# Two-block transformer on one core: the adaptive shift leaves the first three projections and comes back as a bias

## The reference, cut to what matters

```python
mod = (silu(c) @ w_ada + b_ada)            # 6 x 1024 values from one vector c
shift1, scale1, gate1, shift2, scale2, gate2 = split(mod, 6)
h = rms_norm(x, norm1_w) * (1.0 + scale1) + shift1
proj = h @ w_in                            # 11 column blocks of 256, and 16 gate columns
gq, gk, gv, gz, ga, gb, sq, sk, sv = split(proj, ...)
qkv = silu(causal_depthwise_conv(concat([gq, gk, gv]), conv_w))   # four taps
# gated delta rule on q, k, v; sliding window attention on sq, sk, sv; w_out; residual
```

## Time and profile before

| | |
|---|---|
| median of 3 runs | 989.45 us (989.44 to 989.48) |
| profiled execution, its own time | 991.1 us |
| its span | 989.3 us |
| PE busy | 977.1 us |
| DVE busy | 607.5 us |
| ACT busy | 476.9 us |
| DMA, mean over the span | 188 GB/s |

### The profile page before, as it was taken

The page is one execution under the profiler, slowest core; times in us unless marked ns, Lnnn a source line. Parts: engine busy times, 40 slices in busy tenths (PEclk is TensorE's granted clock), DMA queues, the critical chain, the costliest instruction groups (busy, mean ns, idle before and its releaser), DMA issues.

```text
span 989.3 us, 15628 instructions
## 1 busy us (share of the span) xinstructions
PE 977.1 (99%) x6703; PEld 845.5 (85%) x6703; DVE 607.5 (61%) x750; ACT 476.9 (48%) x640; POOL 36.8 (4%) x37
## 2 busy tenths in 40 slices
PE   8999999999999999999999999999999999999998
PEld 6799989978888888999888888889999888888886
DVE  2688987775665454787754545365876663545444
ACT  3485377454343435533364344446655563435343
POOL 0000560010000000000000000000000000000000
PEclk9999999999999999999999999999999999999999
DMA  9857224775767354446544645454643435554621
GB/s 345 310 183 266 97 87 149 272 241 217 276 217 289 129 209 173 169 173 213 213 144 155 213 171 207 176 194 147 231 153 129 140 145 184 182 202 166 217 85 43
DMA packets 31588, 185.70 MB, mean 188 GB/s; under 512 B 3040, under 2 KB 5536, under 8 KB 10784
## 3 DMA queue, kind: packets, MB, share of 16 engines
q1 hardware_dynamic: 29984, 180.37, 50.9%
q0 software_dynamic: 832, 3.17, 1.0%
q10 hardware_dynamic: 704, 1.17, 0.3%
HBM read 183.62 MB, written 1.07 MB: 187 GB/s over the span
## 4 chain that ended last, share of the span: by engine, by line
PE 96%; DVE 2%; DMA 1%; ACT 0%; issue 0%; SPq 0%; DVEq 0%
PE bank L1708 50%; PE acc L1708 42%; PE bank L2313 1%; DMA X_inv<-stream 1%; PE bank L2091 1%; PE bank L1804 0%; PE acc L1804 0%; PE acc L2091 0%; PE bank L2171 0%; SPq L566 0%; DVE norm_tmp L1125 0%; PE bank L1984 0%; DVE inv_b L1393 0%; DVE norm_tmp L1513 0%; DVE silu_and_hid L1512 0%
## 5 line engine op out<-in xcount | busy, mean ns | idle before, releaser
L1076 DVE TENSOR_TENSOR w_lo<-raw,w_hi 128x2048 fp32r<-128x2048 f32 x144 | 326.9, 2288 | 146.7 <-ACT w_hi L676 146.6
L1708 PE MATMUL bank<-w_hi,h_parts 128*128 128x512 f32 x1056 | 333.5, 391 | 1.3 <-DVE h_parts L1154 1.3
L676 ACT ACTIVATE w_hi<-raw 128x2048 fp32r<-128x2048 f32 x144 | 271.4, 1909 | 101.8 <-PE acc L1708 70.9
L1708 PEld LDWEIGHTS bank<-w_hi,h_parts 128*128 128x128 f32 x1056 | 198.2, 188 | 44.6 <-issue 1.9
L1708 PE MATMUL bank<-w_lo,h_parts 128*128 128x512 f32 x528 | 205.5, 389 | 0.0
L1708 PE MATMUL acc<-h_parts,w_hi 128*128 128x256 f32 x928 | 169.6, 285 | 1.8 <-DVE h_parts L1129 0.9
L1708 PEld LDWEIGHTS acc<-h_parts,w_hi 128*128 128x128 f32 x928 | 142.1, 188 | 6.7 <-issue 3.3
L1708 PE MATMUL acc<-h_parts,w_lo 128*128 128x256 f32 x464 | 130.5, 281 | 0.0
L1708 PE MATMUL acc<-w_hi,o_hi 128*128 128x512 f32 x296 | 119.1, 402 | 0.0
L1708 PEld LDWEIGHTS bank<-w_lo,h_parts 128*128 128x128 f32 x528 | 99.2, 188 | 19.8
L1708 PE MATMUL acc<-w_hi,o_lo 128*128 128x512 f32 x296 | 115.6, 391 | 0.0
(11 more groups left out here) (370 smaller groups left out, 992.4 us busy)
## 6 DMA issues: line engine op xcount, KB each, us to landing
raw<-stream SPq DMA_DIRECT2D x162, 1024.0 KB, 5.1
AT<-stream SPq DMA_DIRECT2D x2, 1024.0 KB, 12.2
qkT<-stream SPq DMA_DIRECT2D x2, 1024.0 KB, 13.4
X_inv<-stream SPq DMA_DIRECT2D x2, 1024.0 KB, 14.3
keys_queries<-stream SPq DMA_DIRECT2D x4, 512.0 KB, 12.7
t_tables<-t_scratch POOLq DMA_DIRECT2D x1, 2048.0 KB, 10.6
x_res<-x_in SPq DMA_DIRECT2D x2, 512.0 KB, 5.1
t_tables<-t_scratch POOLq DMA_DIRECT2D x1, 1024.0 KB, 12.9
```

The source lines that it names most:

```text
L676: act.activation(high_of(w), raw_of(r), ACT.Copy).then_inc(s.hi_ready, 1)
L1076: dve.tensor_tensor(low_of(w), raw_of(weight_load(w)), high_of(w), ALU.subtract).then_inc(s.lo_ready, 1)
L1708: return pe.matmul(o, l, r, start=start, stop=stop, skip_group_check=True)
```

## The change

Since h = x * a1 + shift, h @ w = (x * a1) @ w + shift @ w, and the second term is one number per output column. Projections 0 to 2 (`BIASED`) are now made from the scaled rows without the shift, and shift @ w is added when the product is copied into the convolution's pads.

- Loads: the four pieces of scale come first, w0 and w1 between them, then w2, then the four pieces of shift. w3 and w4 (`ASIDE`) land in two of the `ada_raw` buffers. w5, w6 and w7 go into the three raw slots, each after its slot's bias product.
- `scaled_high` and `scaled_low` make the parts of x * a1; `scale_rows` keeps x * a1 itself. When the shift is there `h_high` and `first_low` overwrite the parts with those of h, for projection 3 onwards and for the gate columns.
- The first half of the shift is summed by `ada`; the second on VectorE (`accumulate_shift`, eight instructions on 128 x 512).
- `bias_part` multiplies the shift by the raw weights of w0 to w2 (six calls of four matmuls), two copies on ScalarE, `bias_sums`, and a copy into `bias`. `last_columns` is gone, `warm` falls from 46 matmuls to 31.
- w2 and w3 are split by quarters too. There are two pads and two convolution sums. The gate columns' product moves ahead of projection 3.
- Later: `project(8)` moves ahead of the rows `kb01`, `kb23`, `q01`; `kq_sums` 0 and 1 move into projection 7. On VectorE `accumulate` of m8, m9, m10 and m11 and `lo(10)` move as shown.

```diff
-FIRST_WEIGHTS = 2
+FIRST_WEIGHTS = 4
+BIASED = 3
+ASIDE = 2
...
+            load_ada(0)
+            load_ada(1)
             load(0)
             load(1)
-            for i in range(4):
-                load_ada(1, i)
-            sp.wait_ge(ada_landed[2], 32)
-            for i in range(2, len(LOADS)):
+            load_ada(2)
+            load_ada(3)
+            load(2)
+            for i in range(4, 8):
+                load_ada(i)
+            for i in range(3, len(LOADS)):
                 load(i)
...
+            def accumulate_shift(i):
+                dve.wait_ge(ada_landed[2 + i], 32)
+                for k in range(4):
+                    piece, c = ada_raw[2 + i][:, 512 * k:512 * k + 512], c_act[:, 4 * i + k:4 * i + k + 1]
...
+                    ins = dve.scalar_tensor_tensor(out=shift_acc, in0=piece, scalar=c, in1=shift_acc, op0=ALU.mult, op1=ALU.add)
...
+            accumulate_shift(0)
+            first_shifts(0)
+            for k in range(4):
+                first_low(k)
+            accumulate_shift(1)
             first_shifts(1)
...
+            def bias_part(w, half):
+
+                for k in range(4):
+                    ins = mm(bias_bank(w)[32 * k:32 * k + 32, :], shift_columns[:, 4 * half + k, :], raw_of(w)[:, 4 * half + k, :],
+                             half == 0 and w != 1, half == 1)
+                return ins
...
+            column_part(0, range(0, 4))
+            column_part(1, range(0, 2))
+            ada(2)
+            column_part(1, range(2, 4))
+            ada(3)
+            warm(2)
+            pe.wait_ge(s.rows_copied, 2)
+            row_sums(1, mod_rows[1])
+            column_part(2, range(0, 4))
+            ada(4)
+            column_part(0, range(4, 6))
+            ada(5)
+            column_part(0, range(6, KD)).then_inc(s.block_used, 1)
+            column_part(1, range(4, KD)).then_inc(s.block_used, 1)
+            pe.wait_ge(s.rows_copied, 3)
+            row_sums(2, mod_rows[2])
+            column_part(2, range(4, 6))
+            pe.wait_ge(s.shift_dve, 1)
+            for w in range(BIASED):
+                bias_part(w, 0)
+            pe.wait_ge(s.shift_dve, 2)
+            row_sums(3, shift_acc)
+            column_part(2, range(6, KD)).then_inc(s.block_used, 1)
+            pe.wait_ge(s.gab_lo, 1)
+            gab_part(range(0, 4))
+            pe.wait_ge(s.shift_dve, 3)
+            for w in range(BIASED):
+                bias_part(w, 1).then_inc(s.bias_product, 1)
+            gab_part(range(4, KD)).then_inc(s.gab_product, 1)
+            bias_sums()
+            column_part(3, range(0, 4))
...
-            lo(8)
             at = MOD_START[1]
-            accumulate(at)
-            at += 1
             dve.wait_ge(s.head_sums, 1)
             link(dve.tensor_scalar(hs[:, 0, :], STAT[:, 64:96], EPS, None, ALU.add))
             dve.reciprocal(hs[:, 1, :], hs[:, 0, :]).then_inc(s.head_inv, 1)
-
+            lo(9)
             hsv = hs[:, 2, :].rearrange("p (t c) -> p t c", t=TT)
             dve.wait_ge(s.head_rms, 1)
...
-            lo(9)
+            accumulate(at)
+            at += 1
...
             row_scale("q01", qT[:, 0:2, :], qT[:, 0:2, :])
-
-            accumulate(at)
-            at += 1
-            lo(10)
-            accumulate(at)
-            at += 1
             row_scale("q23", qT[:, 2:4, :], qT[:, 2:4, :])
...
             for gi in range(3):
                 decay(gi)
-
+            accumulate(at)
+            at += 1
             decay(3)
+            lo(10)
             accumulate(at)
             at += 1
...
             for gi in range(4):
                 wait_big(f"qk{gi}")
                 big_read(f"qk{gi}", dve.tensor_tensor(qkT[:, gi, :], big(f"qk{gi}")[:, :], DT[:, gi, :], ALU.mult))
+            accumulate(at)
+            at += 1
...
-            project(6, first_sums)
+            project(6)
+            project(7, first_sums)
             kq_sums(2)
             kq_sums(3).then_inc(s.head_sums, 1)
-            project(7)
+            project(8)
...
             rows("q01", at(coefq), (0, 1))
-            project(8)
             rows("q23", at(coefq), (2, 3))
```

More of the change, by code:

```diff
@@ L549, in load @@
             def load(i):
[L550 to L570, removed]
@@ L749, in feature, with pad_rows @@
                     act.activation(head_sq[w].rearrange("p (a b) -> p a b", a=2), dest[w], ACT.Square).then_inc(s.head_squared, 1)
[L751 to L754, removed]
+            def pad_rows(w):
                 act.wait_ge(s.block_used, w + 1)
[L756 to L772, removed]
@@ new lines, in pad_rows @@
+                if w >= 2:
+                    act.wait_ge(s.conv_done, w - 1)
+                if w >= BIASED:
+                    act.activation(pads[w % 2][:, :, 3:259], A[w % 4].rearrange("p (a b) -> p a b", a=2), ACT.Copy).then_inc(s.pad_ready, 1)
+                    return
+                for mt in range(2):
+                    act.activation(pads[w % 2][:, mt, 3:259], A[w][:, 256 * mt:256 * mt + 256], ACT.Identity,
+                                   bias=bias[:, 2 * w + mt:2 * w + mt + 1]).then_inc(s.pad_ready, 1)
@@ new lines, in _ @@
+            for k in range(4, KD):
+                scaled_low(k)
+            first_lows(2, (2, 3))
+            accumulate_shift(0)
[3 more added lines that the diff above has]
+            accumulate_shift(1)
+            first_shifts(1)
+            first_low(4)
+            first_low(5)
+            first_lows(3, (0, 1))
+            first_low(6)
+            first_low(7)
+            first_lows(3, (2, 3))
+            dve.wait_ge(s.rows_summed, 5)
@@ new lines, in conv @@
+                        dve.wait_ge(s.dve_step, steps[0] - 1)
+                        ins = dve.scalar_tensor_tensor(out=o, in0=pad[:, mt, tap:tap + 256], scalar=vec[:, cw:cw + 1],
+                                                       in1=o, op0=ALU.mult, op1=ALU.add)
+                        if tap == 3 and mt == 1:
+                            dve.wait_ge(s.dve_step, steps[0])
+                            ins.then_inc(s.conv_done, 1)
+                        else:
+                            ins.then_inc(s.dve_step, 1)
+                            steps[0] += 1
@@ new lines, in row_sums, with bias_sums @@
+                    ins = by_halves(STAT[:, at:at + WIDE], rows[:, P * j:P * j + P], ones.broadcast_to([P, WIDE]), True, True)
+                ins.then_inc(s.rows_summed, 1)
+            def bias_sums():
+                pe.wait_ge(s.rows_copied, 5)
+                pe.wait_ge(s.mod_ready, 4)
+                for j in range(2 * BIASED):
+                    at = WIDE * j
+                    ins = by_halves(STAT[:, at:at + WIDE], bias_rows[:, P * j:P * j + P], ones.broadcast_to([P, WIDE]), True, True)
```

433 lines of the change are left out of this document (244 added, 189 removed).

## The result

| | before | changed |
|---|---|---|
| median | 989.45 us (989.38 to 989.48, 5 runs) | 1000.16 us (999.96 to 1000.41, 5 runs) |
| span of the profiled execution | 989.3 us | 998.6 us |

The ratio is 1.0102, 95% interval [1.0091, 1.0113]: 10.7 us slower. The direction was forecast, with about half of the size (+5.4), and the time lies above the range (990.5 to 998.5).

The account below looks back on a forecast made before the run. TensorE, busy 977 of 989 us, was taken to bound the kernel; 0.7 gained at the start and delays in VectorE's list summed to +5.4, span 994.7, time 994.8. Own range 993.3 to 996.3, full range 990.5 to 998.5.

Parts of the forecast that it names:

- first product: TensorE's first product at the start, claimed at 18.0 us, six us earlier than before.
- `bias_part` at 0.45: Bias products at the start, 0.45 us each; first three covered by the shift wait, last three on the path at 1.35.
- the shift wait in place of the old one: Before the shift's row sums, TensorE waits 2.8 us for VectorE's sum of the second half, known at 46.0.
- the late w10: w10's load, issued at 90.4 instead of 83.0 once m8 frees its slot, lands 5.8 us later at 96.2.
- the wait for `eg`: ScalarE, behind `hi(10)`, reads `eg` at 99.5 instead of 98.2; VectorE's `kbgT` queues behind it, +1.2 us.
- `qk` waiting for the `kk` read: VectorE's first `kk` read at 114.8 instead of 110.65; `qk` on TensorE waits for its banks, TensorE +4.1 us.
- an unbroken tail: From the first inversion update to the end nothing is made up; the same distance as before.
- So I add nothing: Slow TensorE clock after the new waits at 43 and `qk`: priced at nothing and made a rival.
- I take the difference as the same for both.: Profiled execution 991.1, span 989.3, median 989.45: difference taken as equal for both kernels, giving span 994.7, time 994.8.
- The start: TensorE up to projection 4: shift known at 46.0, row sums 46.6, projection 4 at 60.3 against 61.0, gain 0.7.
- Then one accumulation 2.3 … one accumulation 2.3: VectorE between G2's mask (106.7) and the first `kk` read (114.8): two accumulations, each priced at 2.3 us.
- Rival 3: Slow clock after the new waits, at two or three places 0.8 to 1.7 us: 996.5 to 998.5; chance 0.2.

Follow-up runs that it names:

- run 2: Changed kernel with the shift summed in one piece, VectorE doing all eight accumulate_shift instructions before first_shifts(0) and the low parts: 997.41 us, ratio 1.0075.
- run 3: Changed kernel with VectorE's late work reordered (m8 before the head sums, m9 behind the coefficients, lo(10) behind q23, m10 before the last decay): 995.17 us, 1.0047.
- run 9: Both repairs and the first two waits filled, with one accumulation fewer before the softmax (done later), against the changed kernel: 995.91 us, 1.0060.
- run 5: Changed kernel with zero matmuls in all of TensorE's waits (6, 4, 9, 3 and 14), run twice: 997.56 and 997.43 us, the second 1.0072.
- run 6: Changed kernel with both repairs, the shift summed in one piece and VectorE's late work reordered: 990.84 us, ratio 1.0010.
- run 8: Kernel before the change without 22 zero matmuls of its start: 993.02 us, ratio 1.0041.
- run 1: Changed kernel with ten zero matmuls in the shift wait alone: 1001.75 us, ratio 1.0115.
- run 4: Changed kernel with GpSimd scaling only 4 of 512 columns of each decay block, the others left unscaled: 996.93 us, ratio 1.0070.
- 7: Changed kernel with both repairs (shift in one piece, VectorE's late work reordered) and zero matmuls in the first two waits: 990.96 us, ratio 1.0012.
- 11: Run 9 with four more zero matmuls, ahead of the square sums of w_out's last block: 992.73 us, ratio 1.0032.

## Why the forecast was half of the loss

Right, with its size: first product, `bias_part` at 0.45, the shift wait in place of the old one (2.58 for 2.8; without it, in run 2, projection 4 starts 2.4 earlier), the late w10, the wait for `eg`, `qk` waiting for the `kk` read, VectorE as the new bound (run 3: 4.1 back at the first update from the order alone; run 9), an unbroken tail. So the path was right, and what failed are terms of the sum: the clock put at nothing, twice, the start, and the price of an accumulation. Forecast and measured differ by 5.3 us, and it adds up so:

- **"So I add nothing"**, the clock after the shift wait. The spell came and cost 1.1: projection 4 at 63.0, at 61.88 with the waits filled. That after `qk` VectorE covers it was right (run 5).
- **"I take the difference as the same for both."** This is the step I had not doubted. The kernel before took 991.1 in its profiled execution and 989.45 in the median, and that 1.65 was the spell of the earlier trace rows: most later executions of it have spans of 987.6 to 988.5 at a mean clock of 0.999 to 1.000, the others 989.2 to 990.1 at 0.997 to 0.998. The changed kernel has the spell, at 156, in its trace, and its other four executions, with the same mean clock (0.994) and spans within 0.4 us, look the same. So the spans to be compared are some 987.8 and 998.3, and 1.5 was missing from the sum. What such a spell costs is seen behind the first update, too: to the end it is 859.1 to 859.4 us in the traces that have one there (before, changed, 5, 6, 8), and 857.4 to 858.0 in those that have none (1 to 4, 7).
- **The start, 1.6 too late apart from the clock**: the shift's row sums come at 47.07 in run 5 (46.0 forecast), and half a microsecond of that is there by w2's first product (29.60 for 29.1 in the changed kernel); from the row sums to projection 4 it is 14.8, not 14.3.
- **"Then one accumulation 2.3 … one accumulation 2.3"**: mis-sized. Three of them run beside GpSimd at 3.12, 3.13 and 3.30, 2.5 more; the first two, 1.6, stand ahead of the `kk` read. The four subtractions behind them, which GpSimd used to slow, take 2.48 in place of 4.20, which takes back the third and more, and w10 landed 4.9 after its slot was free, not 5.8. From projection 4 to the first update this leaves 76.1 us against 75.2 forecast.
- From the first update to the end 0.2.

Together 1.1 + 1.5 + 1.6 + 0.9 + 0.2 = 5.3. The parts are differences between single traces and spans, good to a few tenths. Rival 3 had the clock as the cause but priced the wrong places: one of its spells was hidden, and the one that counted was in my base.

On the mis-sized accumulations the Trainium skill has a rule that the forecast should have weighed: "SBUF — State Buffer", section "Who interferes with whom", says that VectorE and GpSimd share a port pair as an exclusive lock, that a VectorE instruction with two SBUF inputs contends with a GpSimd instruction that reads SBUF, and that the order of issue decides which of the two is blocked. The traces agree: a norm on GpSimd takes 1.04 where it starts first, as in run 1, where the mask of VectorE that starts 0.17 later takes 1.42 instead of 0.69,

```profile
108.43 1.04 POOL L643 TENSOR_TENSOR X_inv<-X_inv,head_stat 128x512 f32<-128x512 f32 x1 [43.58 <-ACT X_inv L880]
```

and 2.36 where it starts behind `lo(10)`. The accumulation behind `lo(10)` then starts while that norm runs and takes 3.13. In run 4 the accumulations go back to 2.35, and the one at 108.02 in the kernel before, which started first, took 2.34.

What is not settled: which wait is followed by a spell. The same wait of 1.2 us before w2 had one behind it in runs 1 and 2, none in the changed kernel and none in run 6. The shift wait of 2.6 had one behind it in the changed kernel and in run 3, none in run 4, which had one at 19 instead. That zero matmuls matter is shown (runs 5 and 8); that a given number of them at a given place is enough is not (runs 1 and 11). Why the steps of the start took longer than forecast was not tried.

## What to carry to other kernels

Before a sum is made on a profiled execution, subtract what makes it differ from the median: here a slow spell of 1.7 us stood in it, and the changed kernel kept it for good. An earlier start is worth only what the engine that binds later can take over: 1.8 us gained at projection 4 were gone 70 us later, because VectorE's convolutions had to wait for the bias and its list was pushed out of TensorE's shadow. When work is moved on VectorE, look at what GpSimd does at the new place and which of the two starts first, and when waits are removed or added, leave the zero matmuls or expect to pay for the clock.

## What was not expected of the hardware

- 22 zero matmuls left out cost 3.3 us (run 8), and one wait of 0.87 us stood ahead of 13 us at half clock (run 9). Most other spells seen here lasted some 3.4 us, that at `qk` in run 2 some 7, and that at the start of run 8 some 10.
- One accumulation of 128 x 2048 takes 3.12 us where it starts while a multiplication of GpSimd runs, and 2.34 where it starts first (108.02 in the kernel before); then the multiplication takes 2.42 instead of 1.04.
